# Residual written straight into the output, expert sums added to it by accumulating transfers from GpSimd's queue

## What is computed

```python
h = rms_norm(x, pre_norm_ffn[l]) * (1.0 + sc2) + sh2
y = hierarchical_moe(h, ...)              # top-1 group, top-2 experts in it
x = x + g2 * rms_norm(y, post_norm_ffn[l])   # the residual x is called x2 in the kernel
```

## Time and profile before

| | |
|---|---|
| median of 3 runs | 1118.79 us (1117.5 to 1123.71) |
| the profiled execution, in all | 1120.98 us |
| its span in the profile | 1119.2 us |
| TensorE busy | 943.3 us, 84% |
| VectorE busy | 525.0 us, 47% |
| ScalarE busy | 304.6 us, 27% |
| GpSimd busy | 192.2 us, 17% |
| device memory read, written | 174.21 MB, 24.64 MB |

### The profile page before, as it was taken

One profiled execution on the slowest core, in us unless ns is written; L12 is line 12 of the kernel. 1 busy time (PEld: TensorE's weight loads), 2 busy tenths in 40 slices (PEclk: granted clock), 3 DMA queues, 4 the chain that ended last, 5 costly groups with the idle time before them and its releaser, 6 DMA issues. The chain is left out here.

```text
span 1119.2 us, 12144 instructions
## 1 busy us (share of the span) xinstructions
PE 943.3 (84%) x4218; PEld 501.3 (45%) x4218; DVE 525.0 (47%) x870; ACT 304.6 (27%) x589; POOL 192.2 (17%) x234
## 2 busy tenths in 40 slices
PE   2599999997889999978858999941999999999944
PEld 1454444443445656657844555541333333333311
DVE  5453437443665555657851443345332333233327
ACT  3220001111444334422321212110333333333313
POOL 5100000222300000003660010000222221222004
PEclk9599999999799999998878999965899999999977
DMA  9963332000000000012004222259599999999547
GB/s 317 376 254 150 150 151 47 1 0 1 0 1 1 1 1 1 1 38 114 1 0 169 100 95 76 94 232 398 195 405 422 388 416 405 409 417 384 194 173 297
DMA packets 47763, 192.35 MB, mean 172 GB/s; under 512 B 14354, under 2 KB 19538, under 8 KB 31186
## 3 DMA queue, kind: packets, MB, share of 16 engines
q1 hardware_dynamic: 40196, 173.10, 39.4%
q0 software_dynamic: 7504, 18.43, 4.6%
HBM read 174.21 MB, written 24.64 MB: 178 GB/s over the span
## 5 line engine op out<-in xcount | busy, mean ns | idle before, releaser
L1584 PE MATMUL PS<-ring,xg_T 128*64 x368 | 163.6, 598 | 4.0 <-DVE near_gu L1948 2.1
L1584 PE MATMUL PS<-near_gu,xg_T 128*64 128x512 f32 x368 | 163.6, 598 | 0.0
L1512 PE MATMUL PS<-w_out_sb,cat_T 128*128 128x512 f32 x256 | 113.5, 602 | 2.8 <-ACT cat_T L1652 2.8
L739 PE MATMUL PS<-hT,w_in_sb 128*128 128x512 f32 x256 | 112.6, 601 | 1.2 <-DVE hT L578 1.2
L1584 PEld LDWEIGHTS PS<-ring,xg_T 128*64 128x64 f32 x368 | 50.7, 138 | 109.1 <-issue 109.1
L383 POOL TENSOR_SCALAR rstd<-stat 128x1 f32<-128x1 f32 (+1 forms) x48 | 23.0, 480 | 391.8 <-ACT junk L507 197.2
L1610 PE MATMUL PS<-ring,hid_T 128*64 x184 | 83.8, 598 | 0.4 <-DVE hid_T L1937 0.4
L1610 PE MATMUL PS<-near_dn,hid_T 128*64 128x512 f32 x184 | 83.9, 598 | 0.0
L1060 PE MATMUL PS<-kT,qT 96*128 96x512 f32 (+4 forms) x192 | 76.6, 509 | 3.0 <-ACT qT L851 3.0
L1928 DVE TENSOR_TENSOR hid<-PS,hid_s 128x128 f32<-128x128 f32 x46 | 11.3, 286 | 144.5 <-ACT hid_s L1693 144.4
L945 DVE TENSOR_REDUCE row_max<-PS 128x1 f32<-128x1024 f32 (+7 forms) x64 | 48.2, 753 | 63.9 <-PE PS L1062 63.8
(11 more groups left out here) (327 smaller groups left out, 1502.2 us busy)
## 6 DMA issues: line engine op xcount, KB each, us to landing
ring<-in_w_gate_dram SPq DMA_DIRECT2D x32, 1024.0 KB, 9.7
ring<-in_w_up_dram SPq DMA_DIRECT2D x32, 1024.0 KB, 11.8
ring<-in_w_down_dram SPq DMA_DIRECT2D x32, 1024.0 KB, 16.0
ada_later<-in_ada_w_dram SPq DMA_DIRECT2D x16, 1024.0 KB, 4.6
ada_first<-in_ada_w_dram SPq DMA_DIRECT2D x8, 1024.0 KB, 10.5
y_g<-y_rows SPq DMA_DIRECT2D x8, 1024.0 KB, 12.0
x_in<-in_x_dram SPq DMA_DIRECT2D x8, 512.0 KB, 8.4
w_in_sb<-in_w_in_dram SPq DMA_DIRECT2D x4, 1024.0 KB, 12.5
```

What stands on the lines that cost most here:

```text
L739: last = pe.matmul(BANK[4 + n % 4][:, :], w_in_sb[:, k, XC0 + ct * P:XC0 + (ct + 1) * P], hT[:, k, hh * HALF:(hh + 1) * HALF], start=(k == ...
L1512: last = pe.matmul(BANK[2 + t % 2 * 2 + j], cat_T[t % 2][:, k, :], w_out_sb[:, k, j * HALF:(j + 1) * HALF], start=(k == 0), stop=(k == KC ...
L1584: last = pe.matmul(BANK[2 + b][rows_, :], xg_T[b][:, k, rows_], gu[u][:, :, k, :], start=(k == 0), stop=(k == KC - 1))
```

## The change

The scratch tensor `x2_rows` is gone. The residual tiles are stored into the output tensor. They aren't loaded back, and VectorE doesn't add them. After its scaling (`o_scaled`), a tile is sent to the output by GpSimd's queue in a transfer that adds to what stands there. GpSimd issues the one of tile t - 1 after the inverse root of tile t. SyncE still waits for all eight landings at the end.

```diff
--- before.py
+++ after.py
@@ -207,7 +207,6 @@
         x2 = [place(f"x2_{i}", TILE_X2 + 4096 * i, [P, D]) for i in range(2)]
         h2_rows = nc.dram_tensor("h2_rows", [T, D], F32).ap()
         y_rows = nc.dram_tensor("y_rows", [2 * T, D], F32).ap()
-        x2_rows = nc.dram_tensor("x2_rows", [T, D], F32).ap()
 
         w_r = place("w_r", R_S + 16384, [P, KC, NG + E])
         logits = nc.alloc_sbuf_tensor_at("logits", [P, NT, NG + E], F32, offset=FRONT)
@@ -1398,7 +1397,7 @@
                 load_expert(sp, 0, 0)
                 for t in range(NT):
                     sp.wait_ge(S["x2_done"], t + 1)
-                    sp.dma_start(x2_rows[t * P:(t + 1) * P, :], x2[t % 2][:, :]).then_inc(S[f"x2_stored{t % 2}"], 16)
+                    sp.dma_start(out[0, t * P:(t + 1) * P, :], x2[t % 2][:, :]).then_inc(S[f"x2_stored{t % 2}"], 16)
                     sp.wait_ge(S["h2_done"], t + 1)
                     sp.dma_start(h2_rows[t * P:(t + 1) * P, :], h2[t % 2][:, :]).then_inc(S[f"h2_stored{t % 2}"], 16)
                     if t + 2 < NT:
@@ -1439,18 +1438,10 @@
                     load_down(sp, e, r)
                 landed(E - 2)
                 landed(E - 1)
-                used = last_step(E - RING + 2)
-                sp.wait_ge(S["dn_done"], used)
-                for t in range(NT):
-                    sp.dma_start(x2_all[:, t, :], x2_rows[t * P:(t + 1) * P, :]).then_inc(S["x2_back"], 16)
-
                 sp.wait_ge(S["moe_stored"], 1)
                 for t in range(NT):
                     sp.dma_start(y_g[t][:, :, :], y_rows[2 * t * P:2 * (t + 1) * P, :].rearrange("(p j) d -> p j d", j=2))\
                         .then_inc(S[f"yg_loaded{t}"], 16)
-                for t in range(NT):
-                    sp.wait_ge(S["o_done"], t + 1)
-                    sp.dma_start(out[0, t * P:(t + 1) * P, :], y_sum[t][:, :]).then_inc(S["o_stored"], 16)
                 sp.wait_ge(S["o_stored"], 16 * NT)
 
 
@@ -1483,10 +1474,18 @@
                     for b in range(2):
                         pool.wait_ge(S[f"ye_stored{b}"], 16 * len(range(b, hi, 2)))
 
+                def add_out(t):
+
+                    pool.wait_ge(S["o_scaled"], t + 1)
+                    pool.dma_start(out[0, t * P:(t + 1) * P, :], y_sum[t][:, :], accum_op=ALU.add).then_inc(S["o_stored"], 16)
+
                 steps(pool, run)
                 pool.sem_inc(S["moe_stored"], 1)
                 for t in range(NT):
                     inverse_root(pool, 7, t, S["ysum_sq"], t + 1)
+                    if t:
+                        add_out(t - 1)
+                add_out(NT - 1)
 
 
             @block.tensor
@@ -1991,10 +1990,6 @@
                     dve.wait_ge(S["rstd_done"], 5 * NT + t + 1)
                     dve.scalar_tensor_tensor(y, pe_sum(t) if t in PE_TILES else y, rstd[:, 7, t:t + 1], G2[:, :], ALU.mult, ALU.mult)\
                         .then_inc(S["o_scaled"], 1)
-                    dve.wait_ge(S["o_scaled"], t + 1)
-                    if t == 0:
-                        dve.wait_ge(S["x2_back"], 16 * NT)
-                    dve.tensor_tensor(y, y, x2_all[:, t, :], ALU.add).then_inc(S["o_done"], 1)
 
 # ---- launch: one core; inputs and output as the reference has them ----
 _INS = ["x", "c", "positions", "ada_w", "ada_b", "pre_norm_mix", "post_norm_mix", "pre_norm_ffn",
```

## The result

| | before | after |
|---|---|---|
| median of 15 runs | 1121.66 us (1117.32 to 1125.65) | 1126.9 us (1124.25 to 1132.14) |
| ratio, 95% interval | | 1.0057 [1.0039, 1.0075] |
| span of the profiled execution | 1119.2 us | 1129.9 us |
| first y_g load issued to end of span ("the tail") | 39.7 us | 45.4 us |

A forecast was written before the change was run, and what follows sets the result against it. DMA engines, always busy from 1097, were taken as the bound: 1102.7 + 8 x 2.46 + 0.9 = 1123.3 against a span of 1119.2, +4.1 us; on the median 1118.8 + 4.1 = 1122.9 us, range 1116 to 1133.

The forecast's parts named there:

- DMA engines that are full with accumulating transfers until the end: Main case for the tail: accumulating transfers at about 2.46 us a tile set the end, 1120 to 1126 us, chance 0.42.
- Removed loads and the moved residual: Ahead of the tail: dropping eight x2_all loads and storing the residual in the output gains 0, at most 0.2 us.
- The adds: VectorE in the tail: 9.8 us of adds go, 4.9 us in the chain, but y_g7's landing limits the gain.
- chain for a load that isn't delayed: Tile 7 after y_g7 lands at 1102.7: TensorE, square, GpSimd's steps and VectorE's scaling, ending at 1111.6.
- GpSimd's issue: GpSimd's queue in the tail: 1.0 us per accumulating transfer, hidden because tile 7's data comes later.
- The case of GpSimd as the bound: Rival for the tail: issues of 1.95 us between roots make GpSimd set the end, +5.8 us, 1124.6; chance 0.08.
- Price of an accumulating transfer: DMA engines, output tiles: 2.46 us a tile against 1.30 for a plain store.
- The choice among the bounds: Accumulating transfer's price: between 1.30 us (plain store) and 3.76 (no overlap), the reads alone were taken, 2.46 a tile.
- Turn-taking with the loads: DMA queues in the tail: accumulating transfers run beside the y_g loads, so y_g7 lands at about 1106 instead of 1102.7.
- the plain stores don't disturb the loads: SyncE's queue before the change: output stores stand behind the y_g loads, hardly a store packet moving in 1082 to 1099.
- Sum: End of the kernel: loads end at 1102.7, plus 8 x 2.46, plus 0.9, gives 1123.3, +4.1 us on the span.
- 0.9 us from the last data to the end of the span: End of the kernel: after the last data moves, the span was taken to end 0.9 us later, as before the change.

The follow-up runs named there:

- residual_through_output: Kernel before, only with the residual stored in the output and loaded back from there; ratio to before 1.0004, tail 40.0 us.
- adds_gone: Kernel before without VectorE's residual adds and the loads back of the residual, plain stores from SyncE, residual missing from the output; ratio 0.9954, tail 35.3 us.
- seven_stores_moved: Kernel before with its adds; GpSimd issues the plain stores of tiles 0 to 6, SyncE that of tile 7; ratio 1.0010, tail 41.0 us.
- plain_from_gpsimd: Kernel after with plain stores in place of the accumulating ones on GpSimd's queue, residual missing from the output; ratio to before 0.9992, tail 38.7 us.
- accumulate_held: Kernel after, but GpSimd waits until y_g7 has landed before issuing the first accumulating transfer; ratio to before 1.0078, tail 49.9 us.
- stores_moved: Kernel before with its adds, only that GpSimd issues all plain stores, in the order of the kernel after; ratio to before 1.0027, tail 42.6 us.
- accumulate_7_only: Kernel before with the residual passing through the output and only tile 7 accumulated from GpSimd's queue; ratio to before 1.0027, tail 43.3 us.

## Why the prediction was right or wrong, point by point

The median was forecast at 1122.9 with a range of 1116 to 1133; it is 1126.9. Of the 4.0 us between them 2.9 lie in the kernel before, whose median is 1121.66 over 15 runs and was 1118.79 over the three shown. As a change, +4.1 us was forecast and +6.4 (4.4 to 8.4) measured, by the medians +5.2, by the tails +5.7. The prediction gave 0.53 to a change of less than 0.5% and 0.42 to a slower kernel than that. The ratio lies just beyond 0.5%, so the less likely of the two came true, and its interval reaches to both sides. What was forecast as the mechanism, DMA engines that are full with accumulating transfers until the end, is what the profile shows.

1. *Removed loads and the moved residual: 0.* Right. residual_through_output is at 1.0004.

2. *The adds: up to 4.0 us, not 9.8, as the last load takes over.* Right. adds_gone has its tail at 35.3, 4.4 below before. The prediction's chain for a load that isn't delayed has the last scaling end 32.1 us into the tail (1111.6); in adds_gone the last store goes out at 32.2.

3. *GpSimd's issue: 1.0 us, hidden.* Right in size (0.87 to 1.03) and in effect for this kernel: GpSimd waits before the last root and the last issue, and the DMA engines are full meanwhile. The case of GpSimd as the bound falls. Where the DMA engines aren't the bound, an issue can show: it did in seven_stores_moved.

4. *Price of an accumulating transfer: 2.46 us of all DMA engines.* Measured 2.49 in the full queue. The choice among the bounds, that the reads set the price, is borne out in size. That there are two reads for each row is not shown by these rows; they show bytes moved once at 210 GB/s, half the rate of a plain store. The rule of the Trainium skill, "Collectives: The Full Stack", section "The bandwidth ceiling", by which a reduction runs at half the rate of a copy, gave an estimate of 2.6 us, and this trace agrees with it (2.49 us, 210 against 403 GB/s).

5. *Turn-taking with the loads: y_g7 3.3 us later.* The mechanism is right, the size half: 21.2 us after its issue instead of 19.6, so 1.6 us. The first software packets came 4.0 us after the first issue, at 1104.0, 19.5 us into the tail instead of 17.5. The plain stores from GpSimd's queue delay it alike (20.8 in plain_from_gpsimd against 19.7 in adds_gone). In the kernel after the delay doesn't matter for the end, since the DMA engines are busy from 1104.0 to 1126.6 whoever comes first, and accumulate_held, which takes it away, ends later still. The prediction's remark that the plain stores don't disturb the loads holds only up to 1099. From there to 1102.7, 79 packets of 4 KB of the first stores move beside the last loads, and with nothing beside it y_g7 lands after 18.4 us (accumulate_held), not 19.6.

6. *Sum.* Its first part, the end of the data, was forecast at 1122.4, 42.9 us into the tail, and measured at 1126.6, 42.05 into it. So the engines' work was put 0.8 too high. The prediction counted from 1102.7 as the time "where the loads alone end", 23.2 us into the tail, but stores had moved beside them. In accumulate_held, where they are alone, they end at 22.1, and 22.1 + 8 x 2.49 = 42.0 is what was measured. Its last part is the step that was mis-sized: 0.9 us from the last data to the end of the span, taken from the earlier trace rows, where the last transfer is SyncE's. With a last transfer from GpSimd it is 3.3, because GpSimd's drain is over only 2.2 us after the landing. +3.3 for the data and +2.4 for the end make the 5.7. The two misses, -0.8 and +2.4, have opposite signs, so it is in part luck that +4.1 isn't further off.

## What to carry to other kernels

An accumulating transfer moved work from an engine to the DMA engines at twice the price of a plain store here (2.49 against 1.30 us a tile): add up the bytes of the stretch (stores and loads behind each other, the accumulated ones twice), and do it only where that sum stays below the engines' own chain. Early tiles could be accumulated here without loss, but also without a gain clear of noise, and late ones couldn't. The last transfer of this program is better left to SyncE's queue: from GpSimd's the span ended 2.3 to 2.5 us later after the issue of a plain store.

## What was unexpected of the hardware

- GpSimd's drain at the end of a block ended 1.9 to 2.3 us after SyncE had seen GpSimd's last transfer land (after 2.2, stores_moved 2.2, accumulate_held 2.2, plain_from_gpsimd 2.3, accumulate_7_only 1.9). Without such a transfer in the tail it ended 3.9 us after GpSimd's last instruction (before: 1113.6 to 1117.4), hidden behind the last store. What it does in these times no run shows.
- A plain store beside two accumulating transfers got 4 packets in 2.6 us, while y_g loads of 8 KB rows beside them kept 44.9% of the engines in 1104 to 1109.3. The cause of the difference stays open.
- GpSimd issues a plain transfer of 128 rows in 0.54 to 0.67 us and an accumulating one in 0.87 to 1.04. Four issued straight behind one another in accumulate_held overlap in the view, the longest with 1.93 us, and take 3.74 us together, 0.94 each.
- A run took 2.1 us beyond its span on average in the four kernels in which GpSimd issues seven or eight of the stores between its roots (after, plain_from_gpsimd, stores_moved, seven_stores_moved), 2.0 in accumulate_held and 1.7 to 1.8 in all others. The cause isn't known.
